# A mixture-of-experts stage on one core: half of each down product from high and low parts, the low parts made by GpSimd

## The chip, the cores and the metric

The kernel runs on one core of a Trainium2 chip. The metric is the device time of one launch in microseconds (us). The core's engines work side by side and meet at semaphores: TensorE (PE in the profile, with its weight loads as PEld), VectorE (DVE), ScalarE (ACT), GpSimd (POOL) and SyncE (SP), whose queue here issues most of the weight loads.

## The reference

Two transformer blocks run one after the other on 256 tokens of width 1024 in float32. The change touches only the last part of the second block, a mixture of 32 experts of which each token takes two:

```python
hid = (jax.nn.silu(jnp.einsum('nbd,ndf->nbf', xb, expert_w_gate[blk_e]))
       * jnp.einsum('nbd,ndf->nbf', xb, expert_w_up[blk_e]))
yb = jnp.einsum('nbf,nfd->nbd', hid, expert_w_down[blk_e]).reshape(n_blocks * MOE_BLOCK, D)
...
y = jnp.zeros((T, D), x.dtype).at[tok_sorted].add(yb[dest] * w_sorted[:, None])
```

Each expert has two matrices of 1024 x 256 (gate, up) and one of 256 x 1024 (down), 1 MB each.

## The kernel before

The 512 pairs of token and expert are sorted by expert into four blocks of 128 rows (`x_sorted`, turned so that the model dimension lies on the partitions). There are `PAIRS` = 35 pairs of an expert and a block: one for each of the 32 experts and three for experts whose rows reach into a next block. The loop over n runs over these 35; below, "expert n" is such a pair.

What each engine does for expert n:

- SP (`expert_loads_sync`, L3540) loads gate, up and down into six slots of 1 MB, three for even n and three for odd n. Four of them are the slots `weights0` to `weights3` of the ring that the rest of the kernel uses, two are `expert_raw0` and `expert_raw1`. A slot is loaded again once expert n has used it.
- ACT (`expert_high`, L3560) copies gate and up to the type fp32r, which TensorE multiplies in one pass; this is the high part `expert_pair_hi`. DVE (`expert_low`, L3569) takes the difference of the weights and the high part, `expert_pair_lo`. Both run two experts ahead.
- ACT (L3636) copies the expert's block of rows, 1024 columns of high and 1024 of low part, into `x_block`.
- PE makes gate and up in one bank: 8 tiles of the model dimension, and for each three fp32r products of 512 columns (`mm_split`, L253 to L255: high x high, high x low, low x high).
- ACT makes `expert_silu` from the gate half (L3651), DVE makes `expert_hidden` from it, the up half and the pair's weight (L3693).
- PE transposes `expert_hidden` (two products with the identity, L3584), ACT copies the result to `expert_hT` in SBUF (L3656).
- PE makes the down product (L3605): plain float32 products of `expert_hT` and the raw down weights, 2 halves of 512 columns x 2 tiles of the inner dimension. The profile has two records for each, 8 for an expert.
- DVE adds each half to `y_sorted` (L3677).

The order on each engine is that of the code, with no planner. In round n of the loop PE does the transposes of n, the product of n+1, then the down product of n. ACT does silu n, `x_block` n+2, waits for the transposes of n, `expert_hT` n, then the high parts of n+2. DVE does hidden n, the two additions of n-1, then the low parts of n+2. GpSimd has nothing to do in the loop. At the end the four blocks of `y_sorted` are parted into high and low (ACT L3668, DVE L3703) and multiplied back to token order (PE L3614).

Of the kernel before, what the change touches and what calls it, by code (L numbers as in the profile page):

```python
# [8 lines left out]
F32 = mybir.dt.float32  # L9
F32R = mybir.dt.float32r  # L10
# [5 lines left out]
P = 128  # L16
SEQ = 256
TT = SEQ // P
D = 1024
# [91 lines left out]
class WeightRing:  # L111
# [3 lines left out]
    def __init__(self, c):  # L115
        self.c = c
        self.slots = [c.nc.alloc_sbuf_tensor(f"weights{i}", [P, SLOT], F32).ap() for i in range(RING)]
        self.full = [c.nc.alloc_semaphore(f"weights{i}_full") for i in range(RING)]
        self.order, self.index, self.closed = [], {}, False
# [5 lines left out]
    def view(self, name):  # L125
        n = self.index[name]
        return self.order[n][1][0](self.slots[n % RING])

    def wait_ge(self, lane, name):
# [326 lines left out]
def k_tiles(n, width=256):  # L456
    return lambda slot: slot[:, 0:n * width].rearrange("p (k n) -> p k n", n=width)
# [2737 lines left out]
def tail_memory(c, s, mem, early):  # L3195
# [4 lines left out]
    s.logits, s.t_stats = mem.new("logits", TT, 36), mem.new("t_stats", 2, TT, 12)  # L3200
    s.top, s.pick, s.second, s.p_group = (mem.new(name, TT) for name in ("top", "pick", "second", "p_group"))
    s.r_work, s.r_e, s.both, s.place = (mem.new(name, TT, 32) for name in ("r_work", "r_e", "r_both", "r_place"))
    s.hot = [mem.new(f"hot{n}", TT, 32) for n in range(2)]
# [3 lines left out]
    s.past, s.across = mem.new("r_past", BLOCKS - 1, 32), mem.new("r_across", BLOCKS - 1, 32)  # L3207
    s.here, s.own, s.slot_w = (mem.new(name, BLOCKS, 32) for name in ("r_here", "r_own", "r_slot_w"))
    s.pair_w, s.left = mem.new("pair_w", PAIRS), mem.new("r_left", BLOCKS)
    s.block_i, s.late_i = mem.new("block_i", 32, dtype=I32), mem.new("late_i", BLOCKS - 1, dtype=I32)  # L3210
# [20 lines left out]
    on_hT = lambda name, n: c.nc.alloc_sbuf_tensor_at(name, [P, KT, P], F32R, offset=c.hT_at + 4 * n * KT * P, align_bytes=32).ap()  # L3231
    s.x_block = [(on_hT("x_block0_hi", 0), on_hT("x_block0_lo", 1)), mem.split("x_block1", KT, P)]
    more = [mem.new(f"expert_raw{n}", SLOT) for n in range(2)]
    s.e_slots = [*c.ring.slots, *more]
    s.e_full = [c.nc.alloc_semaphore(f"expert_full{n}") for n in range(len(s.e_slots))]
# [336 lines left out]


def experts_tensor(c, s):
    pe, inner, turned, outs = c.moe.pe, c.banks[0:2], c.banks[2:4], c.banks[4:8]
    for b0 in range(0, BLOCKS, 2):
        yield from pe.wait_ge("read", "slot T", b0)
    for n in range(-1, PAIRS):
# [23 lines left out]
        raw = expert_raw(s, "down", n)  # L3602
        for half in range(2):
            for k in range(2):
                ins = pe.e.matmul(outs[2 * (n % 2) + half], s.e_hT[n % 2][:, k * P:(k + 1) * P], raw[:, k, half * 512:(half + 1) * 512],  # L3605
                                  start=k == 0, stop=k == 1)
            ins.then_inc(*pe.mark("expert", "down", n, half))
# [32 lines left out]
def experts_scalar(c, s):  # L3640
# [5 lines left out]
    for n in range(-1, PAIRS):  # L3646
# [7 lines left out]
        if n >= 0:  # L3654
            yield from act.wait_ge("expert", "turned", n)
            act.e.activation(s.e_hT[n % 2], c.banks[2 + n % 2][:, 0:2 * P], ACT.Copy).then_inc(*act.mark("expert", "hidden T", n))  # L3656
        if n + 2 < PAIRS:
            yield from expert_high(c, s, n + 2)
# [113 lines left out]
def make_stages(c):  # L3772
# [7 lines left out]
    c.ahead = Stage(c, "ahead", "tensor scalar")  # L3780
    c.tail, c.moe = Stage(c, "tail", "tensor vector scalar gpsimd"), Stage(c, "moe", "tensor vector scalar")
    c.turn_banks = Banks(c, 4, 5, 0, 1)
# [22 lines left out]
def gpsimd_program(c, s):  # L3805
# [9 lines left out]
    tail_loads_gpsimd(c, s)  # L3815
    yield from route_constants_gpsimd(c, s)


# [63 lines left out]
```

## Time and profile before

| | us |
|---|---|
| median of 3 runs | 1721.13 |
| lowest, highest | 1720.15, 1723.42 |
| the profiled execution | 1725.51 |
| its span from the first to the last instruction | 1724.2 |
| mean granted TensorE clock in it | 0.944 of full speed |
| transposes of expert 0 to transposes of expert 33 | 1385.29 to 1688.15 |

The span has 1.3 us less than the time of its own run. The expert loop lies near the end of the program, from about 1385 to 1702 us, and takes 18% of the span; 22 us follow it. Of the whole span PE is busy 91%, DVE 58%, ACT 45% and POOL 14%.

### The profile page before, as it was taken

The numbers are of one execution on the slowest core, as the hardware profiler recorded it, in microseconds if no ns is written. First come the engines' busy times: TensorE is split into PE (matmuls) and PEld (weight loads), VectorE is DVE, ScalarE is ACT, GpSimd is POOL, SyncE is SP. The second block draws the span as 40 slices with busy tenths as digits, with TensorE's granted clock in tenths as the row PEclk, the third lists the DMA queues.
The fourth block names the chain that finished last, engine by engine and source line by source line (L and its number), as shares of the span: only waits on it lengthen the run. The fifth ranks groups of instructions, "written<-read, shape, count | busy, mean of one in ns | idle before, by whom it ended". The sixth has DMA issues, their size and how long they took to land. (4 is left out here: it accounts for less than half of the span.)

```text
span 1724.2 us, 22798 instructions
## 1 busy us (share of the span) xinstructions
PE 1566.9 (91%) x9435; PEld 1324.0 (77%) x9435; DVE 995.0 (58%) x1254; ACT 772.0 (45%) x1133; POOL 232.9 (14%) x337
## 2 busy tenths in 40 slices
PE   4988899999988899999998888989979899999996
PEld 4977689898877789998987786768867766666664
DVE  6568456666665454445474527683333666666666
ACT  3455265445554354544442213222201376666662
POOL 5421100000242000001880002210002000000000
PEclk9899899999998899999999897889969899999998
DMA  9856168775571055553541130202204279999982
GB/s 348 263 199 208 39 226 289 266 262 204 185 268 37 1 197 193 196 193 120 165 127 69 50 110 25 74 25 74 98 25 153 96 299 339 346 346 337 349 302 93
DMA packets 134589, 310.39 MB, mean 180 GB/s; under 512 B 6239, under 2 KB 99766, under 8 KB 114902
## 3 DMA queue, kind: packets, MB, share of 16 engines
q1 hardware_dynamic: 130326, 299.18, 49.0%
q0 software_dynamic: 3584, 8.71, 2.0%
q8 instruction: 74, 1.21, 0.3%
q10 hardware_dynamic: 576, 1.05, 0.2%
q14 instruction: 29, 0.24, 0.0%
HBM read 307.87 MB, written 1.05 MB: 179 GB/s over the span
## 5 line engine op out<-in xcount | busy, mean ns | idle before, releaser
L318 DVE TENSOR_TENSOR mlp_weights_lo<-weights,mlp_weights_hi 128x2048 fp32r<-128x2048 f32 x64 | 146.4, 2291 | 67.9 <-ACT mlp_weights_hi L308 67.0
L3569 DVE TENSOR_TENSOR expert_pair_lo<-weights,expert_pair_hi 128x2048 fp32r<-128x2048 f32 x53 | 119.8, 2290 | 64.3 <-ACT expert_pair_hi L3560 64.3
L253 PE MATMUL bank<-mlp_in_hi,mlp_weights_hi 128*128 128x256 f32 x512 | 145.0, 283 | 3.6 <-DVE mlp_in_lo L702 3.6
L308 ACT ACTIVATE mlp_weights_hi<-weights 128x2048 fp32r<-128x2048 f32 x64 | 121.9, 1908 | 55.4 <-issue 46.3
L255 PE MATMUL bank<-mlp_in_hi,mlp_weights_lo 128*128 128x256 f32 x512 | 144.9, 283 | 0.0
L254 PE MATMUL bank<-mlp_in_lo,mlp_weights_hi 128*128 128x256 f32 x512 | 144.9, 283 | 0.0
L253 PE MATMUL bank<-expert_pair_hi,x_block_hi 128*128 128x512 f32 x280 | 113.7, 406 | 2.1 <-issue 2.1
L255 PE MATMUL bank<-expert_pair_hi,x_block_lo 128*128 128x512 f32 x280 | 110.3, 394 | 0.0
L254 PE MATMUL bank<-expert_pair_lo,x_block_hi 128*128 128x512 f32 x280 | 110.2, 394 | 0.0
L253 PEld LDWEIGHTS bank<-mlp_in_hi,mlp_weights_hi 128*128 128x128 f32 x512 | 98.2, 192 | 5.0 <-issue 4.0
L2119 PE MATMUL bank<-hT,weights 128*128 128x256 f32 x384 | 98.4, 414 | 3.4 <-ACT rw_bk L2140 1.8
L570 DVE SCALAR_TENSOR_TENSOR ada<-weights,cond,ada 128x2048 f32<-128x2048 f32 x42 | 100.1, 2384 | 2.2 <-DMA weights<-in_w_ada 1.8
L253 PE MATMUL bank<-mlp_weights_hi,hidden_hi 128*128 128x512 f32 x256 | 100.0, 391 | 0.0
L254 PE MATMUL bank<-mlp_weights_lo,hidden_hi 128*128 128x512 f32 x256 | 100.0, 390 | 0.0
L255 PE MATMUL bank<-mlp_weights_hi,hidden_lo 128*128 128x512 f32 x256 | 99.6, 389 | 0.0
L3560 ACT ACTIVATE expert_pair_hi<-weights 128x2048 fp32r<-128x2048 f32 x53 | 99.2, 1906 | 0.0
L254 PEld LDWEIGHTS bank<-mlp_in_lo,mlp_weights_hi 128*128 128x128 f32 x512 | 98.2, 192 | 1.0
L255 PEld LDWEIGHTS bank<-mlp_in_hi,mlp_weights_lo 128*128 128x128 f32 x512 | 98.2, 192 | 0.0
L2119 PEld LDWEIGHTS bank<-hT,weights 128*128 128x128 f32 x384 | 78.0, 208 | 21.4 <-issue 5.6
L1273 DVE TENSOR_TENSOR hidden_lo<-mlp_raw,hidden_hi 128x512 fp32r<-128x512 f32 x32 | 22.1, 692 | 92.4 <-ACT hidden_hi L1252 92.4
L3677 DVE TENSOR_TENSOR y_sorted<-bank,y_sorted 128x512 f32 (+1 forms) x70 | 48.4, 692 | 43.0 <-PE bank L3605 42.5
L1246 ACT ACTIVATE mlp_raw<-bank 128x512 f32<-128x512 f32 x32 | 19.1, 597 | 117.8 <-PE bank L255 117.8
(747 smaller groups left out, 3910.6 us busy)
## 6 DMA issues: line engine op xcount, KB each, us to landing
weights<-in_w_ada SPq DMA_DIRECT2D x48, 1024.0 KB, 5.0
weights<-in_w_in SPq DMA_DIRECT2D x45, 1024.0 KB, 5.1
weights<-in_expert_w_gate SPq DMA_DIRECT2D x35, 1024.0 KB, 4.9
weights<-in_w_up SPq DMA_DIRECT2D x32, 1024.0 KB, 5.4
weights<-in_w_down SPq DMA_DIRECT2D x32, 1024.0 KB, 4.9
weights<-in_expert_w_up SPq DMA_DIRECT2D x18, 1024.0 KB, 6.2
weights<-in_expert_w_down SPq DMA_DIRECT2D x18, 1024.0 KB, 6.9
expert_raw<-in_expert_w_up SPq DMA_DIRECT2D x17, 1024.0 KB, 6.1
```

The lines of the kernel that those rows point to most:

```text
L253: pe.e.matmul(out, lhsT[0], rhs[0], start=start, stop=False)
L254: pe.e.matmul(out, lhsT[0], rhs[1], start=False, stop=False)
L255: return pe.e.matmul(out, lhsT[1], rhs[0], start=False, stop=stop)
L308: act.e.activation(self.of(n)[0], ring.view(name), ACT.Copy).then_inc(*act.mark(*self.key, "high", n))
L318: dve.e.tensor_tensor(lo, ring.view(name), hi.bitcast(F32), SUB).then_inc(*dve.mark(*self.key, "low", n))
L570: dve.e.scalar_tensor_tensor(part, ring.view(name), s.cond[:, k:k + 1], part, MULT, ADD).then_inc(*dve.mark(*name))
L1246: act.e.activation(s.raw, as_cols(c.up_banks.of("up", l, n)), ACT.Relu).then_inc(*act.mark("read", "up", l, n))
L1273: dve.e.tensor_tensor(lo, s.raw, hi.bitcast(F32), SUB).then_inc(*dve.mark("hidden low", l, n))
L2119: ins = pe.e.matmul(bank[:, j * SEQ:(j + 1) * SEQ], w[:, k, j * P:(j + 1) * P], c.hT[:, k, :], start=k == 0, stop=k == KT - 1)
L3560: act.e.activation(pair[0][:, :, i * D_EXPERT:(i + 1) * D_EXPERT], expert_raw(s, kind, n), ACT.Copy).then_inc(*act.mark("expert", "high", ...
L3569: dve.e.tensor_tensor(pair[1][:, :, part], expert_raw(s, kind, n), pair[0][:, :, part].bitcast(F32), SUB).then_inc(*dve.mark("expert", "lo ...
L3677: dve.e.tensor_tensor(part, c.banks[4 + 2 * (n % 2) + half].unsqueeze(1), part, ADD).then_inc(*dve.mark("expert", "added", n, half))
```

## The change

For the second half of the columns (512 to 1023) the down product becomes three fp32r products per tile instead of one float32 product:

- ACT makes a second copy of the transposed hidden rows in fp32r (`expert_hT_hi`), and from the down weights' second half the high part `down_hi`, 1024 columns, in one buffer. Both stand between `expert_hT` n and the high parts of n+2.
- GpSimd gets a program for the loop, `experts_gpsimd`: the low part of the hidden rows (256 columns) and the low part of the down weights' second half (1024 columns), which is written over the raw weights in their slot. `low_view` and `lows` name the slots a second time with the type fp32r for that.
- PE's first half stays as it was; before the second half it waits for both low parts.
- The low and high parts of the hidden rows lie on memory that the router used before.

```diff
@@
+def down_high_scalar(c, s, n):
+
+    act = c.moe.act
+    wait_raw(s, act, "down", n)
+    if n:
+        yield from act.wait_ge("expert", "down", n - 1, 1)
+    act.e.activation(s.down_high, expert_raw(s, "down", n)[:, :, 512:1024], ACT.Copy).then_inc(*act.mark("expert", "down high", n))
+
+
+def experts_gpsimd(c, s):
+
+    pool = c.moe.pool
+    for n in range(PAIRS):
+        yield from pool.wait_ge("expert", "hidden high", n)
+        hT, pair = s.e_hT[n % 2], s.e_hT_pair[n % 2]
+        pool.e.tensor_tensor(pair[1], hT, pair[0].bitcast(F32), SUB).then_inc(*pool.mark("expert", "hidden low", n))
+        yield from pool.wait_ge("expert", "down high", n)
+        half = expert_raw(s, "down", n)[:, :, 512:1024]
+        pool.e.tensor_tensor(expert_down_low(s, n), half, s.down_high.bitcast(F32), SUB).then_inc(*pool.mark("expert", "down low", n))
@@ def experts_tensor(c, s):
         for half in range(2):
+            out = outs[2 * (n % 2) + half]
+            if half:
+                yield from pe.wait_ge("expert", "hidden low", n)
+                yield from pe.wait_ge("expert", "down low", n)
             for k in range(2):
-                ins = pe.e.matmul(outs[2 * (n % 2) + half], s.e_hT[n % 2][:, k * P:(k + 1) * P], raw[:, k, half * 512:(half + 1) * 512],
-                                  start=k == 0, stop=k == 1)
+                if half:
+                    low = expert_down_low(s, n)[:, k, :]
+                    ins = mm_split(pe, out, [v[:, k * P:(k + 1) * P] for v in s.e_hT_pair[n % 2]], (s.down_high[:, k, :], low),
+                                   k == 0, k == 1)
+                else:
+                    ins = pe.e.matmul(out, s.e_hT[n % 2][:, k * P:(k + 1) * P], raw[:, k, 0:512], start=k == 0, stop=k == 1)
@@ def experts_scalar(c, s):
             act.e.activation(s.e_hT[n % 2], c.banks[2 + n % 2][:, 0:2 * P], ACT.Copy).then_inc(*act.mark("expert", "hidden T", n))
+            act.e.activation(s.e_hT_pair[n % 2][0], c.banks[2 + n % 2][:, 0:2 * P], ACT.Copy).then_inc(*act.mark("expert", "hidden high", n))
+            yield from down_high_scalar(c, s, n)
```

ACT's instructions in one round of the loop, before. `expert_pair_hi` are the high parts of gate and up, `x_block` the copies of the rows:

```order
L3636 ACTIVATE x_block_lo<-x_sorted_lo 128x1024
L3656 ACTIVATE expert_hT_293<-bank 128x256 [waits moe_tensor]
L3560 ACTIVATE expert_pair_hi<-weights 128x8x256 [waits expert_full3]
L3560 ACTIVATE expert_pair_hi<-expert_raw_316 128x8x256 [waits expert_full4]
L3651 ACTIVATE expert_silu_251<-bank 128x256 [waits moe_vector,moe_tensor]
```

And in the changed kernel, where the line numbers differ:

```order
L3686 ACTIVATE x_block_lo<-x_sorted_lo 128x1024
L3706 ACTIVATE expert_hT_297<-bank 128x256 [waits moe_tensor]
L3707 ACTIVATE expert_hT_hi<-bank 128x256
L3601 ACTIVATE down_hi<-expert_raw_321 128x1024 [waits expert_full5]
L3577 ACTIVATE expert_pair_hi<-weights 128x8x256 [waits expert_full3]
L3577 ACTIVATE expert_pair_hi<-expert_raw_320 128x8x256 [waits expert_full4]
L3701 ACTIVATE expert_silu_255<-bank 128x256 [waits moe_vector,moe_tensor]
```

Two instructions stand newly between the copy of the transposed rows and the high parts of gate and up.

PE's instructions at the end of a round, before: the last product of gate and up, the down product and the next transposes.

```order
L255 MATMUL bank<-expert_pair_hi,x_block_lo 128x512
L3605 MATMUL bank<-expert_raw_317,expert_hT_293 128x512 [waits expert_full5,moe_scalar]
L3605 MATMUL bank<-expert_raw_317,expert_hT_293 128x512 x3
L3584 MATMUL bank<-identity,expert_hidden_290 128x128 [waits moe_vector]
```

The same place in the changed kernel, where L262 to L264 are `mm_split`:

```order
L264 MATMUL bank<-expert_pair_hi,x_block_lo 128x512
L3656 MATMUL bank<-expert_raw_321,expert_hT_297 128x512 [waits expert_full5,moe_scalar]
L3656 MATMUL bank<-expert_raw_321,expert_hT_297 128x512
L262 MATMUL bank<-down_hi,expert_hT_hi 128x512 [waits moe_gpsimd]
L263 MATMUL bank<-expert_raw_lo,expert_hT_hi 128x512
L264 MATMUL bank<-down_hi,expert_hT_lo 128x512
L262 MATMUL bank<-down_hi,expert_hT_hi 128x512
L263 MATMUL bank<-expert_raw_lo,expert_hT_hi 128x512
L264 MATMUL bank<-down_hi,expert_hT_lo 128x512
L3626 MATMUL bank<-identity,expert_hidden_294 128x128 [waits moe_vector]
```

Two float32 products gave way to six fp32r products, and the first of these waits for GpSimd.

## Rows read from the trace of the kernel before

**Rows 1.** Busy time in a stretch: PE, PEld, DVE, ACT, POOL, clock, DMA, GB/s.

```profile
1500.00:1550.00 50.00, 50.00 (x183) 33.26 (x183) 35.09 (x29) 33.61 (x33) 0.00 (x0) 1.00 0.91 343
```

**Rows 2.** Chain of waits in order of time, 1565 to 1588: start, us, what.

```profile
1565.66 3.43 PE bank L3605 x8
1569.09 0.22 PE bank L3584 x2
...
1574.76 3.43 PE bank L3605 x8
...
1584.01 3.43 PE bank L3605 x8
```

**Rows 3.** Waits from 1390 to 1700: us in total, times, longest.

```profile
DVE expert_pair_lo L3569 <- ACT expert_pair_hi L3560: 55.9, 33, 3.5
```

**Rows 4.** Timeline of ACT, 1541 to 1551.5: start, duration, instruction, idle before, releaser.

```profile
1541.75 0.39 ACT L3656 ACTIVATE expert_hT<-bank 128x256 f32<-128x256 f32 x1 [1.38 <-PE bank L3584]
1542.03 1.91 ACT L3560 ACTIVATE expert_pair_hi<-weights 128x2048 fp32r<-128x2048 f32 x1
1543.83 1.91 ACT L3560 ACTIVATE expert_pair_hi<-expert_raw 128x2048 fp32r<-128x2048 f32 x1
1547.34 0.38 ACT L3651 ACTIVATE expert_silu<-bank 128x256 f32<-128x256 f32 x1 [1.60 <-PE bank L255]
1547.62 1.05 ACT L3636 ACTIVATE x_block_hi<-x_sorted_hi 128x1024 fp32r x1
```

**Rows 5.** Timeline of DVE, the same round.

```profile
1541.64 0.69 DVE L3677 TENSOR_TENSOR y_sorted<-bank,y_sorted 128x512 f32 x1 [0.99 <-PE bank L3605]
1543.97 2.29 DVE L3569 TENSOR_TENSOR expert_pair_lo<-weights,expert_pair_hi 128x2048 fp32r<-128x2048 f32 x1 [1.64 <-ACT expert_pair_hi L3560]
...
1548.38 0.48 DVE L3693 SCALAR_TENSOR_TENSOR expert_hidden<-expert_silu,pair_w,bank 128x256 f32<-128x256 f32 x1
```

**Rows 6.** Timeline of all engines, transposes of one round.

```profile
1541.33 0.38 PE L3584 MATMUL bank<-identity,expert_hidden 128*128 128x128 f32 x2
```

**Rows 7.** Timeline, expert 0 of the loop.

```profile
1384.76 0.47 DVE L3693 SCALAR_TENSOR_TENSOR expert_hidden<-expert_silu,pair_w,bank 128x256 f32<-128x256 f32 x1
...
1385.29 0.44 PE L3584 MATMUL bank<-identity,expert_hidden 128*128 128x128 f32 x2 [1.01 <-DVE expert_hidden L3693]
...
1386.49 0.38 ACT L3656 ACTIVATE expert_hT<-bank 128x256 f32<-128x256 f32 x1
```

**Rows 8.** Timeline of ACT, expert 33.

```profile
1688.57 0.39 ACT L3656 ACTIVATE expert_hT<-bank 128x256 f32<-128x256 f32 x1 [3.27 <-PE bank L3584]
```

**Rows 9.** GpSimd's instructions of four lines: ns least/median/most, first and last start.

```profile
L1007 POOL TENSOR_TENSOR conv<-conv,taps x36: 722/738/2881, 57.1 to 491.4; 128x256 f32<-128x256 f32 x36
...
L2867 POOL TENSOR_TENSOR distance<-distance,s_sin x4: 1262/1313/1357, 1048.1 to 1133.1; 128x512 f32<-128x512 f32 x4
...
L1955 POOL TENSOR_TENSOR rw_shift<-rw_z x14: 611/648/2684, 824.6 to 873.3; 128x256 f32<-128x256 f32 x14
...
L1648 POOL TENSOR_TENSOR xs_d<-xs,d_skip x4: 1034/1356/1481, 133.2 to 525.6; 128x512 f32<-128x512 f32 x4
```

**Rows 10.** Timelines of POOL and DVE, 826 to 830.

```profile
826.31 0.64 POOL L1959 TENSOR_TENSOR rw_low<-rw_shift,rw_z 128x256 f32<-128x256 f32 x1
827.02 2.54 POOL L1955 TENSOR_TENSOR rw_shift<-rw_z 128x256 f32<-128x256 f32 x1
...
826.34 2.75 DVE L318 TENSOR_TENSOR input_weights_lo<-weights,input_weights_hi 128x2048 fp32r<-128x2048 f32 x1 [1.86 <-ACT input_weights_hi L308]
```

**Rows 11.** Timelines of POOL and DVE, 1159 to 1161.

```profile
1159.10 1.92 POOL L2865 TENSOR_SCALAR chunk_start<-distance 128x512 f32<-128x512 f32 x1 [24.77 <-ACT distance L2952]
...
1159.40 0.69 DVE L2433 TENSOR_TENSOR scan_Z<-bank,scan_Z 128x512 f32<-128x512 f32 x1 [0.20 <-PE bank L2420]
```

**Rows 12.** Timelines of ACT and POOL, 1045 to 1049: a wait of GpSimd for ACT.

```profile
1045.06 0.90 ACT L2952 ACTIVATE distance<-time,s_th 128x256 f32<-128x256 f32 x2
...
1046.05 1.94 POOL L2865 TENSOR_SCALAR s_sin<-distance 128x512 f32<-128x512 f32 x1 [34.71 <-ACT distance L2952]
```

**Rows 13.** Timeline of PE, after the last down product.

```profile
1708.19 0.50 PE L3614 MATMUL bank<-y_sorted_hi,slot_T 128*128 128x512 f32 x1 [0.48 <-DVE y_sorted_lo L3703]
```

**Rows 14.** DMA issues from 1400 to 1700: count, KB each, median us to landing.

```profile
weights<-in_expert_w_down SPq DMA_DIRECT2D x16, 1024.0 KB, 6.8
```

More of the change, by code:

```diff
@@ L116, in __init__ @@
         self.c = c
-        self.slots = [c.nc.alloc_sbuf_tensor(f"weights{i}", [P, SLOT], F32).ap() for i in range(RING)]
+        self.slots, self.lows = [], []
+        for i in range(RING):
+            at = c.nc.sbuf_base + -c.nc.sbuf_base % 32
+            self.slots.append(c.nc.alloc_sbuf_tensor(f"weights{i}", [P, SLOT], F32).ap())
+            self.lows.append(c.nc.alloc_sbuf_tensor_at(f"weights{i}_lo", [P, SLOT], F32R, offset=at, align_bytes=32).ap())
         self.full = [c.nc.alloc_semaphore(f"weights{i}_full") for i in range(RING)]
@@ L127, in view, with low_view @@
         return self.order[n][1][0](self.slots[n % RING])
+    def low_view(self, name):
+        n = self.index[name]
+        return self.order[n][1][0](self.lows[n % RING])
     def wait_ge(self, lane, name):
@@ L3201, in tail_memory @@
     s.top, s.pick, s.second, s.p_group = (mem.new(name, TT) for name in ("top", "pick", "second", "p_group"))
+    s.scratch_at = mem.at
     s.r_work, s.r_e, s.both, s.place = (mem.new(name, TT, 32) for name in ("r_work", "r_e", "r_both", "r_place"))
@@ L3208, in tail_memory @@
     s.here, s.own, s.slot_w = (mem.new(name, BLOCKS, 32) for name in ("r_here", "r_own", "r_slot_w"))
+    s.scratch_end = mem.at
     s.pair_w, s.left = mem.new("pair_w", PAIRS), mem.new("r_left", BLOCKS)
@@ L3232, in tail_memory @@
     s.x_block = [(on_hT("x_block0_hi", 0), on_hT("x_block0_lo", 1)), mem.split("x_block1", KT, P)]
+    raw_at = mem.at + -mem.at % 8
     more = [mem.new(f"expert_raw{n}", SLOT) for n in range(2)]
+    again = Region(c, raw_at, mem.at)
+    s.e_lows = [*c.ring.lows, *(again.new(f"expert_raw{n}_lo", SLOT, dtype=F32R) for n in range(2))]
+    s.down_high = mem.new("down_hi", 2, 512, dtype=F32R)
+    scratch = Region(c, s.scratch_at, s.scratch_end)
+    s.e_hT_pair = [scratch.split(f"expert_hT{n}", D_EXPERT) for n in range(2)]
     s.e_slots = [*c.ring.slots, *more]
@@ L3571, in expert_low, with expert_down_low @@
         dve.also("expert", "used", kind, n)
+def expert_down_low(s, n):
+    return k_tiles(2, D)(s.e_lows[expert_slot("down", n)])[:, :, 512:1024]
+def down_high_scalar(c, s, n):
[13 more added lines that the diff above has]
+        pool.e.tensor_tensor(expert_down_low(s, n), half, s.down_high.bitcast(F32), SUB).then_inc(*pool.mark("expert", "down low", n))
 def experts_tensor(c, s):
@@ L3780, in make_stages @@
     c.ahead = Stage(c, "ahead", "tensor scalar")
-    c.tail, c.moe = Stage(c, "tail", "tensor vector scalar gpsimd"), Stage(c, "moe", "tensor vector scalar")
+    c.tail, c.moe = Stage(c, "tail", "tensor vector scalar gpsimd"), Stage(c, "moe", "tensor vector scalar gpsimd")
     c.turn_banks = Banks(c, 4, 5, 0, 1)
@@ L3816, in gpsimd_program @@
     yield from route_constants_gpsimd(c, s)
+    yield from experts_gpsimd(c, s)
 def sync_program(c, s, out):
```

## The prediction

> **What bounds the kernel now.** Only the expert loop and the few microseconds behind it are touched, so I read its stretch first. In it PE is busy for 50.00 of 50 us at a granted clock of 1.00, which is the level of 2.4 GHz [rows 1]. The chain of waits agrees: it stays on PE, product after product, and the down product, 3.43 us, comes every 9.10 or 9.25 us [rows 2]. From the transposes of expert 0, 1385.29 [rows 7], to those of expert 33, at 1688.57 - 0.42 = 1688.15 [rows 8] (0.42 is the distance from transposes to ACT's copy, 1541.33 to 1541.75 [rows 4, 6]), are 302.86 us or 33 rounds of **9.18 us**. PE alone sets them.
>
> The second view is the timeline of the two engines that prepare PE's operands, because a PE that is made faster soon waits for the next slowest thing. There is one ring of waits through all of them. Let T be the start of the transposes of expert n. ACT's copy starts at T + 0.42, the high part of gate 0.28 later [rows 4]. DVE starts the low part of gate 1.94 after that (1542.03 to 1543.97), and, the low part of up being in between, starts `expert_hidden` of n+1 another 4.41 later (1543.97 to 1548.38) [rows 4, 5]. PE can start the next transposes 0.53 after that start (1384.76 to 1385.29, where PE stood idle for it) [rows 7]. Sum: 0.42 + 0.28 + 1.94 + 4.41 + 0.53 = **7.58 us**. The ring has 1.60 us of slack under PE's 9.18. DVE waits for ACT in each round [rows 3], so all that is put ahead of the high parts on ACT goes straight into the ring.
>
> **PE's work.** The first half keeps two of the four float32 products: 3.43 / 2 = 1.72 us. The second half's two (1.72) become six fp32r products of 512 columns. These are of the form of the 24 in the product of gate and up. A round less its down product is 9.10 - 3.43 = 5.67 or 9.25 - 3.43 = 5.82, less 0.22 for the transposes [rows 2] leaves 5.45 or 5.60 for 24, so 0.23 each, and 6 x 0.23 = 1.38. PE saves 0.34 us in a round, to **8.84 us**. If nothing else changed, 35 rounds would give 12 us.
>
> **ACT's work.** The fp32r copy of the transposed rows has the form of the copy before it and costs the ring 0.28, the distance to the next start. `down_hi` has 1024 columns, like `x_block`: a duration of 1.05, and 0.95 to the next start (1547.62 to the second `x_block` copy; the two copies of 2048 columns start 1.80 apart and last 1.91, the same overlap of 0.1) [rows 4]. Both are ahead of the high parts, so the ring gets 0.28 + 0.95 = 1.23: 7.58 + 1.23 = **8.81 us**. That alone is as long as PE's new round. ACT's rest is covered: high parts end at about T + 5.6, and silu waits for the product, which ends at about T + 5.8. The wait that `down_hi` has for the down product of n-1 is met before the transposes of n, on the same engine's order. The wait for the down weights is new on ACT, with the high parts queued behind it: SP issues that load when PE ends the down product of n-2, at T - 9.2, it lands 6.8 later [rows 14], at T - 2.4, and is wanted at T + 0.98, so 3.4 us are left.
>
> **GpSimd's work, and what it does to DVE.** GpSimd starts about 0.1 after ACT ends (1045.96 to 1046.05) [rows 12]. The low part of the hidden rows, 256 columns, needs about 0.6 to 0.7 [rows 9] and runs from T + 1.2 to T + 1.9, before `down_hi` is there. `down_hi` starts at T + 0.98, ends at T + 2.03, and the low part of the down weights starts at T + 2.13. Its length D is the unknown: no GpSimd instruction of 1024 columns with two inputs is in the trace. The nearest rows are of two kinds. Where the result is written over an input, 256 columns take 0.722 at the least and 512 take 1.262 (lines 1007 and 2867); a line through both gives 2.11 ns a column and 1.262 + 512 x 2.11 ns = **2.34 us** for 1024. Where it goes elsewhere, 0.611 and 1.034 (lines 1955 and 1648) give 1.65 ns and 1.88 us [rows 9]. The new one writes over its input, so I take 2.34; the ends are 1.88 and, twice the 1.36 of a slow 512, 2.7. PE needs this result only for its second half, at T + 0.22 + 5.5 + 1.72 = T + 7.5; it is there at T + 4.5, so PE never waits for GpSimd directly.
>
> DVE does. When DVE began a low part at 826.34 while a GpSimd subtraction was running until 826.95, DVE's took 2.75 instead of 2.29; and the next GpSimd instruction, begun while DVE was at it, took 2.54 where its own length is 0.61, to 0.47 after DVE's end [rows 9, 10]. So an instruction of either engine that reads two inputs from SBUF stands until the other's is through; the cost to DVE was GpSimd's end less DVE's start (0.61), less 0.15 = 0.46. DVE's additions and `expert_hidden` read PSUM and one SBUF tile, and such an addition kept its 0.69 beside GpSimd's work [rows 11], so only the low parts can be caught. (The Trainium skill, "SBUF — State Buffer", section "SBUF: two separate sides", calls this an exclusive lock on a port pair, taken by a DVE instruction with two SBUF inputs against a GpSimd one that reads SBUF, held for the whole instruction. By that rule, which the trace bears out, moving work from DVE to GpSimd isn't free: the rule speaks against this change.)
>
> In a round DVE wants to start the low part of gate at T + 0.42 + 0.28 + 1.23 + 1.94 = T + 3.87. GpSimd holds until T + 2.13 + D. The loss is 2.13 + D - 3.87 - 0.15 = D - 1.89, and the ring becomes 8.81 + D - 1.89: with 2.34, **9.26 us**. The breakeven with 9.18 is D = 2.26, that with PE's 8.84 is D = 1.92. (The Trainium skill, "GPSIMD Engine Reference", section "Reconciling with measured numbers", gives 4497 ns for 2048 columns; an estimate of half, 2.25, would give a round of 9.17 and with the ends below a time 1.4 us over before, so no change that can be told. No run here shows that length.)
>
> **The ends.** In the first round ACT's copy is late, 1386.49 instead of 1385.71 [rows 7], which before was covered by PE and is on the ring now: +0.78. The round from 33 to 34 has no low parts, so PE bounds it: -0.34. After the last transposes, ACT's two new instructions stand ahead of the high parts of `y_sorted`, on which DVE's low parts and then PE's last products wait (PE idle 0.48 for them [rows 13]): +1.23. DVE's load and all else behind stay.
>
> **The sum.** 33 rounds x (9.26 - 9.18) = +2.7; +0.78 - 0.34 + 1.23 = +1.67; together +4.4 us. The profiled execution, 1725.51 with a span of 1724.2, would be 1729.9; it stood 4.4 above the median of the three runs. The median goes from 1721.1 to **1725.5**. In general the difference is 33 x (D - 2.26) + 1.7.
>
> **Not bounds.** DMA carries 343 GB/s at a share of 0.91 [rows 1]; a round no shorter than 9.18 asks no more of it. Slots of gate and up come free about as late as the ring, with a round to spare. The clock stayed at 1.00 with PE always busy; PE would now idle 0.4 us in a round of 9.3, and I take no loss.
>
> **Rivals.**
> - **GpSimd is quick** (D at or below 2.1, or its instruction leaves DVE alone). Then the ring is 8.81 to 9.0 and PE's saving shows. At D = 1.88 the round is 8.84: 33 x -0.34 = -11.2, with the ends -9.7, so 1711.4. For it: the 1.88 of the second kind of rows, and that what tells the kinds apart (writing in place) is my guess. Against: both in-place rows. It decides below D = 2.1.
> - **GpSimd is slower or caught itself**: the operands are two runs of 512 columns, not one, or something holds its start. D = 2.7 or a start 0.35 late gives a round of 9.62: +14.5 + 1.7, so 1737. Beyond that DVE's second low part would not be hit, as GpSimd has one long instruction in a round.
> - **The ring is as long as PE was** (D about 2.2): 1721 to 1724, no change that can be told. This is also where a change that didn't reach the timeline would end, but each added instruction is in the order.
>
> **How the numbers follow.** The forecast (D from 2.2 to 2.5, 1721 to 1731) gets 0.52, of which 0.34 lies more than 0.2% (3.4 us, about what a measurement of this kernel can tell from no change) above and 0.18 within; quick 0.21; slower GpSimd 0.19; about 2.1 to 2.2 or no effect, 0.08. So faster 0.21, same 0.26, slower 0.53. The range goes from D = 2.0 (33 x -0.26 + 1.7 = -6.9, and a little more for a ring read too long, 1713) to D = 2.65 (+14.6, 1736).
>
> **What would show it.** Right: rounds of 9.2 to 9.4 us; PE idle ahead of the transposes for `expert_hidden`; the first low part in each round 2.6 to 2.9 us instead of 2.29 and the second 2.29; GpSimd's 1024 columns 2.2 to 2.5; the down product 3.1 us. Wrong: rounds of 8.84 with PE full; low parts of 2.29 beside a running GpSimd; PE waiting for GpSimd or for ACT's `expert_hT`; a clock below 1.00 in the loop.

## The result and the profile after

The changed kernel takes 1729.0 us (median of 12 runs, 1727.1 to 1736.0) against 1720.05 for the kernel before (12 runs beside it): a ratio of 1.0052 with a 95% interval of 1.0039 to 1.0064, so **8.9 us slower**. The forecast of +4.4 had the right sign, and 1729.0 lies within the forecast range, but +4.4 is half of the size.

The profiled execution of after has a span of 1734.3 us, 10.1 more than before's 1724.2. I divide it at the transposes of expert 0 and of expert 33, which start at 1387.42 and 1697.22 in after.

| part of the span | before | after | difference | forecast |
|---|---|---|---|---|
| up to the transposes of expert 0 | 1385.29 | 1387.42 | +2.1 | 0 |
| round 0 | 9.21 | 9.93 | +0.7 | +0.86 |
| the next 32 rounds | 32 x 9.177 | 32 x 9.371 | +6.2 | +2.6 |
| from the transposes of expert 33 | 36.05 | 37.08 | +1.0 | +0.9 |

The first part runs unchanged code. One stretch of it, as both traces have it (busy time of PE, PEld, DVE, ACT, POOL, granted clock, DMA share, GB/s), before and then after:

```profile
1040.00:1050.00 10.00, 9.94 (x120) 7.96 (x120) 2.50 (x6) 4.10 (x9) 3.20 (x2) 0.67 0.01 2
```

```profile
1040.00:1050.00 10.00, 10.00 (x115) 8.88 (x114) 2.17 (x6) 3.56 (x7) 2.62 (x2) 0.50 0.01 2
```

PE was full in both, at a granted clock of 0.67 in the one and 0.50, the level of 1.2 GHz, in the other. The offset of 2.1 us arises about there: DVE's instructions start 0.3 earlier in after around 973 and 2.6 later around 1147. I count it as a difference of these two executions and not as an effect of the change: in the runs below, whose code ahead of the loop is the same, ACT's first `expert_hT` copy starts anywhere from 1377.67 (shift_one) to 1388.46 (after). So the change costs about 8 us in this pair of traces, which agrees with the interval of the medians (+6.7 to +11.0).

Nearly all of the rest, 6.9 us, is in the rounds. The same two views of after, first the stretch that [rows 1] has of before:

```profile
1500.00:1550.00 50.00, 48.33 (x194) 34.69 (x194) 35.67 (x28) 39.67 (x44) 17.07 (x12) 1.00 0.88 341
1550.00:1600.00 50.00, 48.66 (x196) 35.05 (x195) 35.85 (x26) 40.42 (x42) 17.65 (x11) 1.00 0.88 343
```

PE is no longer full: 48.33 of 50 us instead of 50.00. The clock is still 1.00 (the level of 2.4 GHz), and DMA carries 341 GB/s for 343. The page's shares of the chain that ended last, before and after:

```profile
PE 40%; DVE 6%; ACT 1%; issue 1%; ACTq 0%; DVEq 0%
PE bank L3605 7%; PE bank L2119 5%; PE bank L283 4%; PE bank L253 4%; PE bank L255 4%; PE bank L254 4%; PE bank L2420 2%; PE bank L1068 2%; PE bank L2887 1%; PE bank L2921 1%; PE bank L2534 1%; DVE expert_pair_lo L3569 1%; PE bank L3584 0%; PE bank L261 0%; PE bank L3289 0%
```

```profile
PE 23%; DVE 16%; ACT 7%; issue 2%; DVEq 0%; ACTq 0%
DVE expert_pair_lo L3586 10%; PE bank L2128 5%; PE bank L292 4%; ACT expert_pair_hi L3577 3%; PE bank L2429 2%; ACT down_hi L3601 2%; PE bank L1077 2%; PE bank L2896 1%; PE bank L2930 1%; PE bank L3626 1%; DVE expert_hidden L3745 1%; ACT expert_hT_hi L3707 1%; PE bank L2543 1%; PE bank L270 1%; PE bank L262 1%
```

The low parts of gate and up (L3586) are now the costliest line of the chain, with 10%; before it was the down product (L3605) with 7%, and they had 1% (L3569). In order of time (start, us, what), one turn of the chain in after, where [rows 2] has only PE:

```profile
1556.67 0.45 PE bank L3626 x2
1557.12 0.02 issue
1557.14 0.03 ACT expert_hT L3706
1557.17 0.25 issue
1557.42 0.38 ACT expert_hT_hi L3707
1557.80 0.95 ACT down_hi L3601
1558.74 1.81 ACT expert_pair_hi L3577
1560.56 0.02 issue
1560.58 5.00 DVE expert_pair_lo L3586 x2
1565.58 0.40 DVE expert_hidden L3745
1565.99 0.04 issue
1566.03 0.45 PE bank L3626 x2
```

This is the ring of the prediction, piece by piece, from one pair of transposes to the next: 1566.03 - 1556.67 = 9.36 us. The product of gate and up and the down product aren't in it.

The timeline of the round before it, start, duration, instruction, then in brackets the idle time ahead of it and its releaser, shows who holds DVE (left out: PE's products, DVE's additions, silu, `x_block` and the loads):

```profile
1547.30 0.44 PE L3626 MATMUL bank<-identity,expert_hidden 128*128 128x128 f32 x2 [0.34 <-DVE expert_hidden L3745]
1547.77 0.39 ACT L3706 ACTIVATE expert_hT<-bank 128x256 f32<-128x256 f32 x1 [1.61 <-PE bank L3626]
1548.05 0.38 ACT L3707 ACTIVATE expert_hT_hi<-bank 128x256 fp32r<-128x256 f32 x1
1548.32 1.06 ACT L3601 ACTIVATE down_hi<-expert_raw 128x1024 fp32r<-128x1024 f32 x1
1548.51 0.74 POOL L3610 TENSOR_TENSOR expert_hT_lo<-expert_hT,expert_hT_hi 128x256 fp32r<-128x256 f32 x1 [6.01 <-ACT expert_hT_hi L3707]
1549.27 1.92 ACT L3577 ACTIVATE expert_pair_hi<-weights 128x2048 fp32r<-128x2048 f32 x1
1549.46 2.41 POOL L3613 TENSOR_TENSOR expert_raw_lo<-expert_raw,down_hi 128x1024 fp32r<-128x1024 f32 x1 [0.21 <-ACT down_hi L3601]
1551.22 2.80 DVE L3586 TENSOR_TENSOR expert_pair_lo<-weights,expert_pair_hi 128x2048 fp32r<-128x2048 f32 x1 [2.17 <-ACT expert_pair_hi L3577]
1553.94 2.28 DVE L3586 TENSOR_TENSOR expert_pair_lo<-expert_raw,expert_pair_hi 128x2048 fp32r<-128x2048 f32 x1
1556.14 0.47 DVE L3745 SCALAR_TENSOR_TENSOR expert_hidden<-expert_silu,pair_w,bank 128x256 f32<-128x256 f32 x1
1556.67 0.44 PE L3626 MATMUL bank<-identity,expert_hidden 128*128 128x128 f32 x2 [0.22 <-DVE expert_hidden L3745]
```

GpSimd's low part of the down weights runs until 1549.46 + 2.41 = 1551.87. DVE's first low part starts at 1551.22, while it runs, and takes 2.80 instead of [rows 5]'s 2.29; the second starts after it and takes 2.28. The waits from 1395 to 1710 (us in total, times, longest) say that PE now waits for DVE once in each round:

```profile
PEld bank L3626 <- DVE expert_hidden L3745: 24.1, 33, 1.3
...
PE bank L3626 <- DVE expert_hidden L3745: 9.9, 33, 0.9
```

### The profile page after: what moved, and what is told of

Same layout as the page of the kernel before. It is cut to its first block and busy times, and to the rows that moved or that the text cites. A ratio compares the mean times of both kernels' runs of the same rounds, so it can differ in the third digit from the quotient of the medians.

```text
span 1734.3 us, 23113 instructions
## 1 busy us (share of the span) xinstructions
PE 1565.6 (90%) x9505; PEld 1336.4 (77%) x9505; DVE 1011.9 (58%) x1254; ACT 814.5 (47%) x1203; POOL 342.8 (20%) x407
## 3 DMA queue, kind: packets, MB, share of 16 engines
q8 instruction: 75, 1.23, 0.3%
## 5 line engine op out<-in xcount | busy, mean ns | idle before, releaser
L3586 DVE TENSOR_TENSOR expert_pair_lo<-weights,expert_pair_hi 128x2048 fp32r<-128x2048 f32 x53 | 136.8, 2606 | 82.2 <-ACT expert_pair_hi L3577 82.2
L262 PE MATMUL bank<-mlp_in_hi,mlp_weights_hi 128*128 128x256 f32 x512 | 145.0, 283 | 3.6 <-DVE mlp_in_lo L711 3.6
L264 PE MATMUL bank<-mlp_in_hi,mlp_weights_lo 128*128 128x256 f32 x512 | 144.9, 283 | 0.0
L262 PE MATMUL bank<-expert_pair_hi,x_block_hi 128*128 128x512 f32 x280 | 113.8, 406 | 1.9 <-issue 1.9
L264 PE MATMUL bank<-expert_pair_hi,x_block_lo 128*128 128x512 f32 x280 | 110.6, 395 | 0.0
L262 PEld LDWEIGHTS bank<-mlp_in_hi,mlp_weights_hi 128*128 128x128 f32 x512 | 98.2, 192 | 5.0 <-issue 3.9
L262 PE MATMUL bank<-mlp_weights_hi,hidden_hi 128*128 128x512 f32 x256 | 100.0, 391 | 0.0
L264 PE MATMUL bank<-mlp_weights_hi,hidden_lo 128*128 128x512 f32 x256 | 99.6, 389 | 0.0
L264 PEld LDWEIGHTS bank<-mlp_in_hi,mlp_weights_lo 128*128 128x128 f32 x512 | 98.1, 192 | 0.0
L3610 POOL TENSOR_TENSOR expert_hT_lo<-expert_hT,expert_hT_hi 128x256 fp32r<-128x256 f32 x35 | 26.0, 742 | 258.4 <-ACT expert_hT_hi L3707 258.4
```

The costliest lines, as they stand in the source:

```text
L262: pe.e.matmul(out, lhsT[0], rhs[0], start=start, stop=False)
L264: return pe.e.matmul(out, lhsT[1], rhs[0], start=False, stop=stop)
L3586: dve.e.tensor_tensor(pair[1][:, :, part], expert_raw(s, kind, n), pair[0][:, :, part].bitcast(F32), SUB).then_inc(*dve.mark("expert", "lo ...
```

## The experiments

Each is a ratio to the kernel before, from runs of both on the same chip. "Rounds" is the mean distance of ACT's `expert_hT` copies from expert 1 to expert 33 in the profiled execution. "Rest" is from the start of expert 33's copy to the end of the span. The profiles differ ahead of the loop by several us from one execution to the next, so rounds are compared first and the medians after.

| kernel | ratio, 95% | low part of down on GpSimd | rounds | rest from copy 33 |
|---|---|---|---|---|
| before | 1 | - | 9.177 | 35.63 |
| after | 1.0052 (1.0039 to 1.0064) | 2.41 | 9.371 | 36.61 |
| no_down_low | 0.9957 (0.9942 to 0.9973) | none | 8.916 | 36.57 |
| write_only | 0.9971 (0.9954 to 0.9987) | 2.99, reads nothing | 8.897 | 38.18 |
| own_place | 1.0041 (1.0021 to 1.0062) | 2.42 | 9.374 | 36.63 |
| early | 0.9953 (0.9936 to 0.9970) | 2.41, moved | 8.861 | 35.66 |
| half_f32 | 1.0075 (1.0057 to 1.0093) | 2.41 | 9.371 | 36.87 |
| cols_896 | 1.0002 (0.9990 to 1.0015) | 2.14 | 9.094 | 36.58 |
| copies_only | 1.0008 (0.9993 to 1.0023) | none | 9.177 | 36.93 |
| shift_one | 0.9964 (0.9951 to 0.9978) | 2.00 | 8.962 | 36.60 |
| early_shift | 0.9954 (0.9935 to 0.9972) | 2.00, moved | 8.926 | 35.69 |
| shift_eight | one run, 1727.33 us | 2.42 | 9.373 | 36.62 |

### no_down_low: the subtraction taken out

```diff
-        half = expert_raw(s, "down", n)[:, :, 512:1024]
-        pool.e.tensor_tensor(expert_down_low(s, n), half, s.down_high.bitcast(F32), SUB).then_inc(...)
...
-                yield from pe.wait_ge("expert", "down low", n)
+                yield from pe.wait_ge("expert", "down high", n)
...
-                    low = expert_down_low(s, n)[:, k, :]
+                    low = s.down_high[:, k, :]
```

> GpSimd's subtraction for the down weights is left out; TensorE multiplies by the high part in its stead. ScalarE's copies and the six fp32r products stay. My theory (VectorE's first low part is held until GpSimd's subtraction ends): that low part takes 2.29 us instead of 2.80, a round 9.37 - 0.51 = 8.86 us instead of 9.37, the time 16 us under the changed kernel and 8 to 9 us under the kernel before. Rival (the round is long because ScalarE's two new copies stand in the ring, or the fp32r products are slower than thought): rounds stay at 9.2 or more and the time at or above that of before.

Rounds of 8.92 and 0.43% faster than before. This one GpSimd instruction costs 0.45 us a round: the 0.19 by which after's rounds are longer than before's, and 0.26 more that the rest of the change would have gained. DVE's low parts of the first kind, as lines have them (count, total and mean ns, idle before):

```profile
L3586 DVE TENSOR_TENSOR expert_pair_lo<-weights,expert_pair_hi 128x2048 fp32r<-128x2048 f32 x47 | 106.3, 2290 | 69.0 <-ACT expert_pair_hi L3577 69.0
```

Their mean is 2290 ns; after's page has 2606 for the same tile, a mean of held ones of 2.80 and, since up lies in a `weights` slot in every second round, free ones of 2.28. The ring is then 9.37 - 0.51 = 8.86, PE's own work 8.84, and the rounds stand a little above both.

### write_only: a GpSimd that is as busy, but reads nothing

The subtraction is replaced by three memsets of the same 1024 columns, so the low part is zero.

```diff
-        pool.e.tensor_tensor(expert_down_low(s, n), half, s.down_high.bitcast(F32), SUB).then_inc(...)
+        for _ in range(3):
+            pool.wait_own()
+            ins = pool.e.memset(expert_down_low(s, n).bitcast(F32), 0.0)
...
```

> GpSimd's subtraction for the down weights is replaced by three memsets over the same 1024 columns, each about 1.0 us, which read nothing (the low part becomes zero). They run from about T + 2.2 to T + 5.3, so longer over VectorE's low parts than the subtraction. If what holds VectorE is only a GpSimd instruction that reads SBUF: low parts 2.29 us, rounds 8.86, time 8 to 9 us under before. If any GpSimd instruction that uses SBUF holds it: the first low part 2.5 to 3.5 us, rounds 9.1 to 9.9, time at or above before.

```profile
1550.54 2.99 POOL L3614 MEMSET expert_raw_lo<- 128x1024 f32 x3 [0.19 <-ACT down_hi L3601]
...
1552.31 2.29 DVE L3586 TENSOR_TENSOR expert_pair_lo<-weights,expert_pair_hi 128x2048 fp32r<-128x2048 f32 x1 [2.16 <-ACT expert_pair_hi L3577]
```

GpSimd writes the same place from 1550.54 to 1553.53, for longer than the subtraction took, and DVE's low part, which starts in the middle, keeps its 2.29 (a mean of 2290 ns in the loop). So it isn't that GpSimd is busy, nor that it writes: here the subtraction's reading is what holds DVE. A GpSimd instruction with one input wasn't tried. The Trainium skill, "SBUF — State Buffer", section "SBUF: two separate sides", says that a DVE instruction with two SBUF inputs contends only with a GpSimd one that reads SBUF; this pair of rows and after's agree with both sides of that.

The run also showed the other end of the loop: its last stretch is 1.6 us longer than after's. PE waits for GpSimd's last low part there, and the products of `y_sorted` behind it are slow:

```profile
1687.12 0.47 PE L262 MATMUL bank<-down_hi,expert_hT_hi 128*128 128x512 f32 x1 [2.36 <-POOL weights_lo L3614]
...
1689.00 0.63 PE L3667 MATMUL bank<-y_sorted_lo,slot_T 128*128 128x512 f32 x1
1689.42 0.63 PE L3667 MATMUL bank<-y_sorted_hi,slot_T 128*128 128x512 f32 x1
```

They start 0.42 apart, at a granted clock of 0.93 from 1680 to 1690 and 0.90 in the 10 us after; in after they start 0.22 apart (1712.26, 1712.48) at 1.00. So most of the 1.6 us is clock, in this one execution, and stands behind a PE that had waited 2.36 us; I haven't tested whether the wait made it.

### own_place: is it the writing in place that makes it slow?

My 2.34 rested on a guess, that the slower rows of [rows 9] are slow because they write over an input. Here the low part goes to a tile of its own (`down_lo`); memory of the router makes room for it, and the high and low parts of the hidden rows share one pair of buffers instead of two.

```diff
...
+    s.down_low = scratch.new("down_lo", 2, 512, dtype=F32R)
...
-    return k_tiles(2, D)(s.e_lows[expert_slot("down", n)])[:, :, 512:1024]
+    return s.down_low
```

> GpSimd writes the low part of the down weights to a tile of its own instead of the weights' place; all else as in the changed kernel. If writing over an input is what makes GpSimd's subtraction slow (1.88 against 2.41 us by the two kinds of rows of before): 1.9 us, VectorE's first low part 2.3, rounds 8.9, time 7 us or more under before. If the place doesn't matter: 2.41 us, 2.80, rounds of 9.37 and the time of the changed kernel, 9 us over before.

GpSimd's instructions of the line, in ns least/median/most, with their first and last start, in after and in own_place:

```profile
L3613 POOL TENSOR_TENSOR weights_lo<-weights,down_hi x18: 2346/2417/2423, 1390.1 to 1708.3; 128x1024 fp32r<-128x1024 f32 x18
```

```profile
L3616 POOL TENSOR_TENSOR down_lo<-weights,down_hi x18: 2343/2420/2423, 1386.4 to 1704.7; 128x1024 fp32r<-128x1024 f32 x18
```

2420 against 2417 ns, and rounds of 9.374 against 9.371. The guess is refuted. A row of after says it too: `expert_hT_lo` (L3610 in its timeline) is written to a place of its own, and its 256 columns take 0.74, about what the rows written in place take (738 in the middle, line 1007 [rows 9]), and not the 0.61 of the other kind.

### shift_one and shift_eight: the start of the second input

If the place of the result doesn't matter, that of the inputs might. In after both inputs start at a multiple of 32 bytes (`Region.new` rounds up to 8 elements). `down_hi` is moved by 4 bytes in one kernel (the diff) and by 32 in the other (`8:1032` instead of `1:1025`); all else stays.

```diff
-    s.down_high = mem.new("down_hi", 2, 512, dtype=F32R)
+    s.down_high = k_tiles(2, 512)(mem.new("down_hi", 1032, dtype=F32R)[:, 1:1025])
```

> The changed kernel with down_hi shifted by one column (4 bytes) in its tile. The two kinds of GpSimd subtractions in the trace of before differ in this too: the quicker ones have an input that starts 4 bytes off. If that is what makes them quick: the subtraction takes 1.9 us instead of 2.41, VectorE's first low part 2.3, rounds 8.9 and a time 7 us or more under before. If not: 2.41, 2.80, 9.37 and 9 us over before. The products that read the shifted operand may take longer than 0.39 us; that would show in the product's records.

> The changed kernel with down_hi shifted by eight columns (32 bytes) instead of one. If the phase within 32 bytes is what counts, GpSimd's subtraction takes 2.41 us as with no shift and the rounds are 9.37; if any distance between the tiles helps, 2.0 us and 8.96.

The same rows, of shift_one and of shift_eight:

```profile
L3613 POOL TENSOR_TENSOR weights_lo<-weights,down_hi x18: 1998/2002/2005, 1379.3 to 1684.0; 128x1024 fp32r<-128x1024 f32 x18
```

```profile
L3613 POOL TENSOR_TENSOR weights_lo<-weights,down_hi x18: 2346/2417/2418, 1381.8 to 1700.1; 128x1024 fp32r<-128x1024 f32 x18
```

Four bytes take the instruction from 2.42 to 2.00 us, and 32 bytes leave it as it was. So the start of an input counts, and whole steps of 32 bytes don't. The rounds follow: DVE's first low part is 2.40 instead of 2.80 and the round 8.962. A change of one line turns 0.5% slower into 0.36% faster. Only these two offsets were tried on `down_hi`.

The trace of before holds more. Each row of `rw_z` has 257 elements, so row k starts 4k bytes past a multiple of 32. Line 1959 adds `rw_z` from element 1 of row k to `rw_shift`, which starts at a multiple of 32: its two inputs lie 4(k + 1) bytes apart. Here k is 7, 1, 2 and 3, so within 32 bytes they lie 0, 8, 12 and 16 apart:

```profile
844.10 0.72 POOL L1959 TENSOR_TENSOR rw_k_in<-rw_shift,rw_z 128x256 f32<-128x256 f32 x1
...
852.12 0.64 POOL L1959 TENSOR_TENSOR rw_r<-rw_shift,rw_z 128x256 f32<-128x256 f32 x1
...
854.62 0.74 POOL L1959 TENSOR_TENSOR rw_r<-rw_shift,rw_z 128x256 f32<-128x256 f32 x1
...
859.09 0.74 POOL L1959 TENSOR_TENSOR rw_r<-rw_shift,rw_z 128x256 f32<-128x256 f32 x1
```

The rows at 4, 20 and 24 bytes take 0.64 too, and all these lengths are the same within 0.01 in the twelve traces. Three of the 14 rows are far longer (1.15 to 2.42), among them the only one at 28, and say nothing of their own length. So 4, 8, 20 and 24 bytes are quick, 0, 12 and 16 are slow, as if it repeated every 16 bytes. Line 1955 always has its inputs 4 bytes apart, while both move with k, and takes 0.61 for k = 0, 2, 4, 5 and 7 (and for 8 and 12): what counts is the distance of the inputs and not where either starts. This parts line 1007 (0, slow) from line 1955 (4, quick) in [rows 9]. It doesn't reach line 1648, whose second input is one value repeated over 64 columns; the expectation's "the quicker ones have an input that starts 4 bytes off" holds for line 1955 alone.

### cols_896: fewer columns

The subtraction covers 896 of the 1024 columns, 448 of each tile, and PE takes the high part in place of the low one for all of them, in as many products as after.

```diff
-        half = expert_raw(s, "down", n)[:, :, 512:1024]
+        half = expert_raw(s, "down", n)[:, :, 512:960]
...
-                    low = expert_down_low(s, n)[:, k, :]
+                    low = s.down_high[:, k, :]
```

> GpSimd subtracts 896 of the 1024 columns of the down weights and TensorE takes the high part in place of the low; all else as in the changed kernel. Theory (the round grows with GpSimd's instruction one for one, from a length of about 1.9 us on): 2.14 us instead of 2.41, VectorE's first low part 2.53 instead of 2.80, rounds 9.10 instead of 9.37, time at that of before. Rival (a fixed cost for each meeting of the two engines): low part 2.8 and rounds 9.37 as before the cut.

2.14 us for 896 columns, and rounds of 9.094. With after and shift_one there are three points: 2.41 gives 9.371, 2.14 gives 9.094, 2.00 gives 8.962. From the first to the second the round falls by 0.277 for 0.27 us, then by 0.13 for 0.14. That is the prediction's formula, one us of round for each us of D.

### half_f32 and copies_only: the two ends of the change

half_f32 has all of the change but its gain: the second half is two float32 products again (of `down_hi`), after the same waits. copies_only is the kernel before with ACT's two copies and nothing that uses them; PE only waits for the second ahead of its second half.

```diff
-                    ins = mm_split(pe, out, [v[:, k * P:(k + 1) * P] for v in s.e_hT_pair[n % 2]], (s.down_high[:, k, :], low),
-                                   k == 0, k == 1)
+                    ins = pe.e.matmul(out, s.e_hT[n % 2][:, k * P:(k + 1) * P], s.down_high[:, k, :].bitcast(F32), ...)
```

> The second half is multiplied in float32 again (two products, with the high part as operand), all else as in the changed kernel, GpSimd and its waits too. Theory (the ring over VectorE sets the round, TensorE's part in it is only the transposes): TensorE's work in a round is 9.18 us again, the ring stays at 9.37, so rounds of 9.37 and the time of the changed kernel, 9 us over before: the 0.33 us saved on TensorE in a round were worth nothing. Rival (TensorE's length still counts): rounds of 9.6 to 9.7, 18 us over before.

```diff
             act.e.activation(s.e_hT[n % 2], c.banks[2 + n % 2][:, 0:2 * P], ACT.Copy).then_inc(...)
+            act.e.activation(s.e_hT_high[n % 2], c.banks[2 + n % 2][:, 0:2 * P], ACT.Copy).then_inc(...)
+            wait_raw(s, act, "down", n)
+            act.e.activation(s.down_high, expert_raw(s, "down", n)[:, :, 512:1024], ACT.Copy).then_inc(...)
```

> The kernel before with ScalarE's two new copies (transposed rows and 1024 columns of the down weights, to fp32r) at their places, their results unused; TensorE waits for the second ahead of its second half; no GpSimd work and no fp32r down products. Theory: the ring is 8.86 us, TensorE's 9.18 still covers it, so rounds of 9.18, and only the end pays: 1.2 us over before. Rival (the copies themselves slow the loop): rounds over 9.3 and 5 us or more over before.

With the 0.34 us of PE given back, half_f32 has rounds of 9.371, those of after to the last digit: within the rounds the saving on PE, for which the change does all else, is worth **nothing**. It is worth something only where no low parts follow: from copy 33 to copy 34 it is 9.25 there and 8.94 in after. By the medians half_f32, with four runs, stands 12.9 us over before (+9.8 to +16.0) and not 9. The rounds don't show the 4 us more, and the last stretch shows 0.3 of it; the intervals of the two kernels overlap, so it isn't shown to be real either. In copies_only the copies alone cost nothing in the rounds (9.177, PE full) and 1.3 us behind them, where they stand ahead of `y_sorted`'s high parts.

### early and early_shift: the order mended

If the ring is what counts, `down_hi` should not stand in it. The down weights lie in their slot before the transposes, so ACT can make the high part while it waits for them. That needs a second buffer (and, as in own_place, one pair of buffers for the hidden rows); GpSimd does the long low part first and the short one of the hidden rows after it. Both orders change at once, so this run doesn't say which of them gives how much.

```diff
+    s.down_high = [s.down_high, scratch.new("down_hi1", 2, 512, dtype=F32R)]
...
-    if n:
-        yield from act.wait_ge("expert", "down", n - 1, 1)
+    if n >= 2:
+        yield from act.wait_ge("expert", "down", n - 2, 1)
...
+            yield from down_high_scalar(c, s, n)
             yield from act.wait_ge("expert", "turned", n)
...
-            yield from down_high_scalar(c, s, n)
...
```

> The high part of the down weights is made one step sooner on ScalarE, ahead of the wait for the transposes (two buffers in dead memory), and GpSimd subtracts the down weights first and the hidden rows' low part second. GpSimd then ends its long subtraction at about T + 3.0 us, as VectorE's first low part begins at about T + 2.95; the short one may hold the second low part by 0.6. Ring 7.9 to 8.5 us, below TensorE's 8.84. Theory: rounds of 8.84, time 10 us under before (ratio 0.994). Rivals: the down weights land too late for ScalarE, which then holds the whole ring (rounds over 9); or the DMA queue, at 345 GB/s before, can't give 356 and the rounds stay at 9.0 to 9.2.

```profile
1550.62 1.05 ACT L3604 ACTIVATE down_hi<-expert_raw 128x1024 fp32r<-128x1024 f32 x1
...
1551.35 0.38 PE L3629 MATMUL bank<-identity,expert_hidden 128*128 128x128 f32 x2
...
1551.76 2.41 POOL L3613 TENSOR_TENSOR expert_raw_lo<-expert_raw,down_hi 128x1024 fp32r<-128x1024 f32 x1 [5.68 <-ACT down_hi L3604]
...
1554.13 0.73 POOL L3616 TENSOR_TENSOR expert_hT_lo<-expert_hT,expert_hT_hi 128x256 fp32r<-128x256 f32 x1
1554.27 2.75 DVE L3589 TENSOR_TENSOR expert_pair_lo<-weights,expert_pair_hi 128x2048 fp32r<-128x2048 f32 x1 [1.65 <-ACT expert_pair_hi L3580]
```

`down_hi` is made ahead of the transposes, and PE goes from product to product without a wait. GpSimd's long low part ends at 1554.17, just ahead of DVE's. DVE is still held, now by GpSimd's short instruction (2.75 at 1554.27), but with 0.95 us taken out of the ring that no longer decides: rounds are 8.861, PE's forecast work of 8.84, and PE is busy for 50.00 of 50 us:

```profile
1500.00:1550.00 50.00, 50.00 (x203) 36.78 (x203) 38.22 (x27) 41.89 (x45) 19.35 (x12) 1.00 0.93 355
```

The rest after expert 33 is as before's (35.66 against 35.63). This is 0.47% faster than before, 1.0% faster than after. DMA has gone up from a share of 0.91 to 0.93. early_shift adds the 4 bytes to it:

> The kernel early, with both buffers of the down weights' high part shifted by 4 bytes. GpSimd's long subtraction takes 2.0 us, ends at about T + 2.5 and is through before VectorE's first low part, so the hidden rows' low part runs before it too. TensorE sets the round in both (8.86 us), so the theory gives no more than early: rounds of 8.86, ratio 0.993 to 0.996, VectorE's first low part 2.3 to 2.5 instead of 2.75. Rival (the meetings of GpSimd and VectorE still cost rounds in early): 8.7 or less a round, 6 us or more under early.

GpSimd needs 2.00 us again, and the time is the same as early's (0.9954 and 0.9953). Its rounds are mostly 8.83 and 8.93 in turn, but some of up to 10.2, each followed by one of about 8.15, bring the mean to 8.926. The trace names what is next:

```profile
1554.85 1.06 ACT L3604 ACTIVATE down_hi<-expert_raw 128x1024 fp32r<-128x1024 f32 x1 [1.46 <-DMA expert_raw<-in_expert_w_down]
```

ACT waited 1.46 us for the down weights; there were 7 such waits in the loop, 5.6 us together, and 2 of 0.8 us together in early. PE is busy for 49.40 to 50.00 of each 50 us from 1400 to 1650. With PE full and the loads just in time, a faster GpSimd has nothing left to give. That the loads came later in this execution than in early isn't explained.

## Why the prediction was right and where it wasn't

- **The bound and its successor: right.** PE's 9.18 gave way to the ring it named, and PE's new round is 8.84 forecast and 8.861 measured in early. The down product takes 3.11 in after (1553.17 to 1556.28) for 3.10. PE is idle ahead of the transposes, for `expert_hidden`, and the clock stayed at 1.00, both as said.
- **ACT's copies: right.** The steps that they add to the ring are 0.27 and 0.95 in after's timeline, for 0.28 and 0.95, free under PE's cover (copies_only) and 1.3 us behind the loop, for 1.23.
- **GpSimd against DVE: right in kind and point.** The first low part is 2.80 in the range of 2.6 to 2.9, the second 2.28; the loss grows with D one for one (three points), and goes away if GpSimd reads nothing (write_only).
- **D: a wrong reason with nearly the right number, by luck.** Of the two kinds of rows I took the slower for their writing in place. own_place refutes that; shift_one and the rows of line 1959 show that the distance of the two inputs' starts makes 2.00 or 2.42. The rows that I took as in place had their inputs 0 apart, as after has, so the right kind was chosen for a reason that had nothing to do with it. By the same mistake the hidden rows' low part was put at 0.6 to 0.7 and takes 0.74, which costs nothing in the ring. The line through the rows of 256 and 512 columns gave 2.34, and 2.41 came. (The Trainium skill, "GPSIMD Engine Reference", section "Reconciling with measured numbers", led to an estimate of 2.25 and to a round of no change; the measured 2.41 is above it, and the 2.00 of the other offset is below it: one figure for this instruction doesn't settle a case with a breakeven of 2.26.)
- **The size, +4.4 for 8.9: the ring was read 0.11 us too short.** From the timeline of after, its terms are 0.47 + 0.28 + 0.27 + 0.95 + 1.95 + 4.92 + 0.53 = 9.37. Two of them are off. The 4.92 was to be 4.41 + 0.45 and is 4.41 + 0.51: that is D, 0.07 longer. The 0.47 from transposes to ACT's copy was to be 0.42, which I had from a round in which PE was full; a PE that comes from idle takes 0.44 for the transposes and not 0.38, and I had that row before me [rows 6, 7]. When one asks for the length of a ring in which PE waits, its pieces must be taken from a place where PE waits. Both are small, but they count 33 times: 33 x 0.11 = 3.6 us, about the loop's +6.9 less the +3.5 forecast for it. The rest of 8.9 - 4.4 lies within the interval of the medians. The forecast for the rounds was 9.26 - 9.18, a small difference of large numbers, and 1.2% of the ring more than doubled it (0.08 forecast, 0.19 measured).
- **PE never waits for GpSimd: wrong at one place.** In the rounds it holds. In the last one no product of gate and up stands between, and PE waits 1.75 us for the last low part:

```profile
1710.80 0.47 PE L262 MATMUL bank<-down_hi,expert_hT_hi 128*128 128x512 f32 x1 [1.75 <-POOL weights_lo L3613]
```

  It costs nothing at 2.41: the rest from copy 33 is 36.61 in after, 36.57 in no_down_low, without that wait, and 36.60 in shift_one, with a shorter one, because `y_sorted`'s last products wait for its high and low parts in any case (PE idle 0.37 us for them in after). With 2.99 (write_only) the wait is 2.36 and the stretch longer, mostly by the clock behind it.
- **The first round and the end: right in size.** +0.7 for +0.86, +1.0 for +0.9.
- **The rivals.** Its sum has a slip: -11.2 with the ends is -9.5 and not -9.7, so 1711.6. "GpSimd is quick" became real 4 bytes away: shift_one at 0.9964 is 6 us faster, for 33 x (2.00 - 2.26) + 1.7 = -6.9 by the formula. "Slower or caught itself" didn't come. Nearest to "the ring is as long as PE was" is cols_896, with a ring of 9.09 for PE's 9.18: 1.0002.

What stays open: why one execution was granted less clock ahead of the loop, and with it some 2 us of the 10.1 between the two profiles; what GpSimd's subtraction needs at distances that neither `down_hi` nor line 1959 shows; and why the loads come just too late in early_shift.

## What to carry to other kernels

Work taken from an engine that is the bound is worth only the distance to the next ring of waits (here 0.34 us of PE, used up before it could show), so write that ring down with each inserted instruction in it, and take its pieces from a place where the engine already waits. In this kernel, what helps the bound engine was better made ahead of the wait that closes the ring, as `early` does, and not behind it, where everything queued on that engine pays. A subtraction that is given to GpSimd is paid for on VectorE where it overlaps VectorE's own subtraction of two SBUF tiles; ask when it ends, not how busy it is.

## What the runs showed of the hardware

- A GpSimd subtraction of 1024 columns takes 2.42 us when both inputs start at the same place within 32 bytes, and 2.00 us when one is moved by 4 bytes; moved by 32 bytes it is 2.42 again. An addition of 256 columns takes 0.64 with the inputs 4, 8, 20 or 24 bytes apart and 0.72 to 0.74 with 0, 12 or 16 (line 1959 of before). PE's products and ACT's copy of the moved tile kept their 0.39 and 1.06 us.
- Written over its input or to a tile of its own, it takes 2.417 or 2.420 us.
- GpSimd's memsets beside a two-input DVE subtraction leave it at 2.29 us; a subtraction there makes it 2.80, or 2.75 with only 0.59 us of the short one (1554.27 to 1554.86) in its way.
